# Gate stage of a two-layer encoder: the low halves of four U blocks on GpSimd, in two parts each, instead of on VectorE

## What is computed

```python
for l in range(DEPTH):                      # 2 layers, 256 tokens, width 1024
    h = _rmsnorm(x, norm_mix[l])
    ...                                     # attention and S5 mixer
    x = x + mix @ w_out[l]
    x = x + _peer(_rmsnorm(x, norm_ffn[l]), w_query[l], sub_keys[l], expert_u[l], expert_v[l])
return _rmsnorm(x, norm_final)

# _peer: 8 heads choose 16 of 16384 single-neuron experts per token
gates = jax.nn.softmax(top_s, axis=-1)
act = jax.nn.gelu(jnp.einsum('td,ted->te', h_c, expert_u[e_c], preferred_element_type=f32), approximate=False)
out = jnp.einsum('te,ted->td', g_c * act, expert_v[e_c].astype(f32))
```

## Time and profile before

| | us |
|---|---|
| median of three runs | 2128.16 |
| lowest, highest | 2127.49, 2131.69 |
| profiled execution, own time | 2125.18 |
| its span in the trace | 2123.4 |
| TensorE busy in the span | 2022.9 (95%) |
| VectorE busy | 1605.3 (76%) |
| GpSimd busy | 695.9 (33%) |

### The profile page before, as it was taken

How to read it: one execution, slowest core, us unless ns; L and a number is a source line. 1 busy time by engine, 2 the same in 40 slices (tenths; PEclk the granted TensorE clock), 3 DMA queues, 4 the chain that set the end, 5 groups by cost and what they waited for, 6 DMA issues and landing times.

```text
span 2123.4 us, 37109 instructions
## 1 busy us (share of the span) xinstructions
PE 2022.9 (95%) x11526; PEld 1679.6 (79%) x11526; DVE 1605.3 (76%) x3087; ACT 989.7 (47%) x1627; POOL 695.9 (33%) x537
## 2 busy tenths in 40 slices
PE   7998999988999999999989999998899999999997
PEld 5764999887887888888867559998778788888886
DVE  6993676887779977777779738778867788777775
ACT  3543454664345444444444435546643544444443
POOL 6992566762000400000059816666600013000000
PEclk9999999999999999999999999999999999999999
DMA  5223454203558555555423235542055665555553
GB/s 195 90 71 144 171 183 160 86 21 119 192 198 292 182 196 187 188 188 187 139 91 102 98 134 189 165 146 71 11 170 195 205 219 182 188 188 190 187 192 112
DMA packets 90971, 330.41 MB, mean 156 GB/s; under 512 B 10452, under 2 KB 14676, under 8 KB 88573
## 3 DMA queue, kind: packets, MB, share of 16 engines
q1 hardware_dynamic: 90860, 329.23, 45.8%
q10 hardware_dynamic: 16, 0.02, 0.0%
HBM read 326.04 MB, written 3.16 MB: 155 GB/s over the span
## 4 chain that ended last, share of the span: by engine, by line
PE 78%; issue 7%; DVE 6%; POOL 4%; DVEq 2%; DMA 1%; ACT 1%; ACTq 0%; SPq 0%; POOLq 0%
PE ps L848 31%; PE ps L811 14%; PE ps L821 12%; PE ps L825 5%; PE ps L609 3%; POOL v_raw L1800 3%; PE ps L858 3%; PE ps L775 3%; DVE arena L1310 2%; PE ps L644 2%; PE ps L626 1%; PE ps L604 1%; DVE arena L1480 1%; DVEq L1730 1%; PE ps L727 1%
## 5 line engine op out<-in xcount | busy, mean ns | idle before, releaser
L848 PE MATMUL ps<-v_hl,w_hl 128*128 128x512 f32 x3072 | 734.2, 393 | 15.4 <-DVE v_hl L1310 15.3
L848 PEld LDWEIGHTS ps<-v_hl,w_hl 128*128 128x128 f32 x3072 | 577.4, 189 | 143.8 <-DVE v_hl L1310 22.5
L821 PE MATMUL ps<-h_hl,u_hl 128*128 128x512 f32 x1152 | 418.3, 397 | 0.0
L1800 POOL TENSOR_TENSOR arena<-arena 128x256 f32<-128x256 f32 (+1 forms) x225 | 213.8, 987 | 371.4 <-DVE arena L1310 368.6
L1310 DVE TENSOR_TENSOR v_hl<-v_raw,v_hl 128x1024 fp32r<-128x1024 f32 x208 | 258.6, 1243 | 49.3 <-ACT v_hl L1143 49.2
L825 PE MATMUL ps<-h_hl,u_hl 128*128 128x256 f32 x1008 | 282.6, 280 | 0.0
L1310 DVE TENSOR_TENSOR u_hl<-u_raw,u_hl 128x1024 fp32r<-128x1024 f32 x148 | 186.6, 1261 | 116.0 <-ACT u_hl L1105 113.7
L1143 ACT ACTIVATE v_hl<-v_raw 128x1024 fp32r<-128x1024 f32 x208 | 218.8, 1053 | 113.4 <-PE ps L848 98.9
L821 PEld LDWEIGHTS ps<-h_hl,u_hl 128*128 128x128 f32 x1152 | 216.4, 188 | 45.1
L1105 ACT ACTIVATE u_hl<-u_raw 128x1024 fp32r<-128x1024 f32 x144 | 152.3, 1058 | 135.3 <-PE ps L821 135.3
L1245 ACT ACTIVATE act_w<-act_w 128x256 f32<-128x256 f32 x144 | 60.2, 418 | 301.6 <-DVE act_w L1745 301.6
(11 more groups left out here) (177 smaller groups left out, 2877.2 us busy)
## 6 DMA issues: line engine op xcount, KB each, us to landing
u_raw<-in_expert_u SPq DMA_DIRECT2D x208, 512.0 KB, 3.3
v_raw<-in_expert_v SPq DMA_DIRECT2D x208, 512.0 KB, 3.3
v_raw<-in_expert_u SPq DMA_DIRECT2D x48, 512.0 KB, 4.4
u_raw<-in_expert_v SPq DMA_DIRECT2D x48, 512.0 KB, 3.3
arena<-in_w_in SPq DMA_DIRECT2D x16, 512.0 KB, 3.8
arena<-in_w_in SPq DMA_DIRECT2D x8, 1024.0 KB, 5.1
arena<-in_ssm_b SPq DMA_DIRECT2D x16, 512.0 KB, 4.7
arena<-in_w_out SPq DMA_DIRECT2D x4, 2048.0 KB, 9.5
```

Source lines behind the costliest of these rows:

```text
L821: return pe.matmul(both, hl[:, 0, k, :], h_hl[:, :, k, :], start=(k == 0), stop=(k == DC - 1))
L848: m = pe.matmul(ps[:, 2 * a + half, :], w_hl[s][:, wp, a * P:(a + 1) * P], v_hl[s][:, vp, half * 512:(half + 1) * 512], start=(first and j ...
L1800: return pool.tensor_tensor(o, a, b, op)
```

## The change

VectorE's `low_ahead` and its table are removed. GpSimd gets `low_part(j, part)`: half of the subtraction, 128x512 elements, placed behind the product of the batches in its own table. The first part waits for the high half, and the second part signals `s_u_lo`. ScalarE's, TensorE's and SyncE's instructions stay as they are, in the same order.

```diff
-                def low_ahead(j):
-                    dve.wait_ge(s_u_hi, l * PK + EARLY + j + 1)
-                    dve.wait_ge(s_u_lo, l * PK + EARLY + j)
-                    tt(early_hl[j % 4][:, 1, :, :], u_raw[j % 2][:, :, :], early_hl[j % 4][:, 0, :, :].bitcast(F32),
-                       ALU.subtract).then_inc(s_u_lo, 1)
...
-                low_after = {2: 4, 6: 5, 14: 6, 24: 7}
                 for t in range(N_BATCH):
...
                     gate_early(t)
-                    if t in low_after:
-                        low_ahead(low_after[t])
...
+                def low_part(j, part):
+                    if part == 0:
+                        pool.wait_ge(s_u_hi, l * PK + EARLY + j + 1)
+                    ks = slice(4 * part, 4 * part + 4)
+                    m = tt(early_hl[j % 4][:, 1, ks, :], u_raw[j % 2][:, ks, :],
+                           early_hl[j % 4][:, 0, ks, :].bitcast(F32), ALU.subtract)
+                    if part:
+                        m.then_inc(s_u_lo, 1)
+
+                low_after = {2: (4, 0), 4: (4, 1), 6: (5, 0), 8: (5, 1), 14: (6, 0), 16: (6, 1), 24: (7, 0), 26: (7, 1)}
                 pool.wait_ge(s_selT, l + 1)
                 for t in range(N_BATCH):
 
                     pool.wait_ge(s_hot1, l * N_BATCH + t + 1)
                     tt(hot1[t % BATCHES], hot1[t % BATCHES], sel_T[:, 2, t * HOT:(t + 1) * HOT].unsqueeze(2)
                        .broadcast_to([P, HOT, PK]), ALU.mult).then_inc(s_gated, 1)
+                    if t in low_after:
+                        low_part(*low_after[t])
```

## The result

| | before | after |
|---|---|---|
| median, us | 2129.93 (4 runs) | 2156.06 (4 runs) |
| span of the profiled execution, us | 2123.4 | 2153.2 |
| first gate stage, us | 102.1 | 116.8 |
| second gate stage, us | 102.1 | 116.4 |

The ratio is 1.012 with a 95% interval of 1.0098 to 1.0142, that is 21 to 30 us. From here on "stage" is the stretch from the start of the first `hot_firsts` to the start of the first down. In that measure the two stages became 28.9 us longer, which is the whole difference of the spans (29.8 us) within 1 us.

A forecast was written before the change was run, and what follows sets the result against it. TensorE bounds the kernel overall, but in the gate stages the chain VectorE, GpSimd, TensorE sets the pace. Delays of 22 us plus 9 us of lowered clock on 2128.2 us give 2159 us; 8-in-10 range 2146 to 2169 us.

The forecast's parts named there:

- batch 5: Gate stage, after block 4's two parts on GpSimd: batch starts at 408.8 against 407.21, 1.6 us later.
- batch 7: Gate stage, after GpSimd's wait for block 5's high half: batch starts at 415.65 against 410.0, 5.6 us later.
- batch 17: Gate stage, after block 6's parts: 2.4 us more delay, on top of 5.1 us from blocks 4 and 5.
- The delays: Gate stage, GpSimd's parts and waits holding up products: 5.1 + 2.4 + 3.45 = 11 us a stage, 22 us for both.
- The waits: GpSimd waiting for ScalarE's high half at each first part: about 0.9, 3.6, 1.1 and 3.4 us.
- The parts' spacing: Time GpSimd needs for one 128x512 part: 1.22 us, between ends of 1.0 and 1.3 us.
- The clock: TensorE at half rate after idle gaps, chiefly before batches 7 and 25: 4.5 us a stage, 9 us for both.
- rival in which the clock falls everywhere: Falls also before batches 3 and 15 and between late batches: another 2 to 6 us a stage, 2163 to 2171 us; chance 0.10.
- The relief of VectorE: VectorE loses four low halves a stage and their waits: about 8.5 us a stage relieved.
- The rival in which the clock stays up: Batches 7 and 25 late, but the gaps leave TensorE's clock alone: 2128.2 + 22 = 2150 us; chance 0.20.
- The rival in which the parts fit into GpSimd's idle time: Gate stage: 9.8 us of parts fit GpSimd's 31.8 us idle, only VectorE's relief counts: 2113 us; chance 0.05.
- Loads at no cost: U loads and SyncE's early loads hang on the later `s_u_lo`, but their blocks are needed late: costed at nothing.

The follow-up runs named there:

- the run with TensorE kept busy: Changed kernel plus 3, 7, 4 and 7 plain matmuls on TensorE ahead of batches 3, 7, 15 and 25: 2148.4 us, ratio 1.0099 to before.
- the run with parts beside the ups: Changed kernel with GpSimd's parts moved behind products 9, 11, 19, 21, 29, 31, 39 and 41: 2120.6 us, ratio 0.9962 to before.

## Why the prediction was right

The forecast of 2159 us stands against 2156.1, slower by 31 us against 26 in the medians and 29 in the stages. By its own steps, with starts counted from the first `hot_firsts` and the mean of both stages:

| step | forecast, against before | after | with the clock kept up |
|---|---|---|---|
| batch 5 | +1.6 | +1.65 | +1.65 |
| batch 7 | +5.6 | +6.25 | +5.8 |
| batch 17 | +7.5, and 3.2 for the clock | +9.9 | +7.8 |
| stage | +11, and 4.5 for the clock | +14.5 | +11.2 |

**The delays** were right to 0.3 us at each place, as the run with TensorE kept busy shows. The waits were forecast as 0.9, 3.6, 1.1 and 3.4 us and are 0.84, 4.12, 1.21 and 3.34 in the first stage (3.66 at block 5 in the second, 3.60 where the clock stays up). The parts' spacing, 1.22 us, was taken from half of the 128x1024 low half and is that. Two experiments from opposite sides, moving the parts or moving the high halves, each removed some 11 of 14.5 us, the clock's share that hangs on the gaps included, so the wait of GpSimd with a product queued behind it is the cause.

**The clock** was the right mechanism and a term that was too large: 4.5 us a stage forecast, 3.2 measured (116.6 less 113.35). Place by place, against the run with the clock kept up and counted at the next batch that shows it (mean of both stages):

| fall at | forecast | measured |
|---|---|---|
| batch 3 | 0 | 0.4 |
| batch 7 and its up | 2.5 | 1.7 |
| batch 15 | 0.7 | 0.5 |
| batch 25 | 1.3 | 0.7 |

At batch 7 I took the length of the low stretch from the end of the gate stage, 5 us into the work. Here it ended 4 us after batch 7's start. The fall before batch 3 was not in the sum. So part of what the large terms had too much was made up by a fall that I had missed, which is luck. It is also half of my rival in which the clock falls everywhere: it did fall before batches 3 and 15, but the two cost 0.9 us a stage together (0.2 more than the sum had for them), not the 2 to 6 us more that the rival asked. The rival in which the clock stays up would have been 2148.4 us by the run that makes it so, and I had put it at 2150.

**The relief of VectorE.** The rival in which the parts fit into GpSimd's idle time does exist, with another table: 0.9962. I priced it at 2113 us from 8.5 us of removed work a stage, of which the ups would hide 1. The run with parts beside the ups has that work removed (8.7 us by the trace) and gives 2120.6, with stages 3.3 us shorter, so 5.4 us did not show. The step of that rival that failed is adding up removed work on an engine that is not the only limit: in that run's first stage VectorE waits 4.8 us longer for TensorE before `gate_early`. In the forecast itself this did no harm, since it was made from start times and not from busy time. VectorE's busy time fell by 5.3 us a stage (the earlier trace rows against the windows after), where I had said about 6.

**Loads at no cost** was right: in the changed kernel no engine waits for a U load in the stage, as the list of waits has only the engines in it.

## What to carry to other kernels

An engine that is idle for a third of a stage may still have no room at the place where work is put on it: look at what is queued behind the new instruction, and who waits for that. Give a wait to the engine that arrives last, or put it behind the last instruction that others need soon; here the same eight instructions were worth -3 or +14 us a stage by their place alone. And price a gap on TensorE with what follows it, because its clock may fall.

## What the runs showed of the hardware

- The clock fell behind gaps that I had thought harmless. In the changed kernel 1.96 us of idle TensorE before batch 3 was followed by a granted clock of 0.50, while TensorE was at work again:

```profile
408.00:409.00 1.00, 0.73 (x6) 1.00 0.00 0
...
411.00:412.00 1.00, 0.84 (x4) 0.50 0.54 164
```

- Where it falls and how long it stays down differs. Behind a gap of 3.25 us before the first down it was low for 5.6 us of the downs in the trace of before (until 505.4); in the run with parts beside the ups for 3.9 us in the first layer (until 502.5) and 5.8 in the second. In the second stage of the changed kernel it was 1.00 through the whole gap of 4.61 us before batch 7 (from 1476 to 1480.6) and 0.50 in the window from 1481 us, when TensorE was already at work. A gap of 1.52 us outside the gate stage (line 626, at 145.2 and 1190.4 us in the run with parts beside the ups) was followed by a fall in the second layer and by none in the first. What decides that, these runs do not show.
- Plain matmuls of 0.46 us each, into a bank that nobody uses, are a cheap way to keep it up: 2.8 us of them in a gap of 3.25 us saved 2.5 us behind it by the medians (1.6 and 2.7 by the traces).
- A GpSimd subtraction of 128x512 with two full operands takes 1.26 to 1.28 us in the changed kernel, and the next instruction starts 1.22 to 1.23 us after its start. VectorE's `hot_firsts` and `hot_second`, which read PSUM and SBUF, beside it take 1.22 and 0.68 us as before.
